# A hybrid mLSTM block on eight cores: weight casts in quarter pieces, branch weights by row blocks, q, k and v weights loaded apart, head 0 on two PSUM banks

## The reference, cut to what matters

```python
D_MODEL, BATCH, SEQ = 1024, 8, 4096          # 4 mLSTM heads of 256; SGU 8 groups x 128; FF 4096
def hybrid_layer(x, mod, ...):
    sh1, sc1, g1, sh2, sc2, g2 = split(mod, 6)           # mod = silu(c) @ w_ada + b_ada
    z = modulate(rmsnorm(x, norm1_g), sh1, sc1) @ w_in   # (S, 8208)
    qk, v_a, o_a, u_b, v_b, mg_pre, if_pre = split(z)    # 2048, 1024, 1024, 1024, 1024, 2048, 16
    qk = silu(centred_conv(qk, conv_w, conv_b))          # 3 taps over the sequence
    hA = mlstm_bidirectional(q, k, v, gates)             # forward scan + backward scan, per head
    y_a = rms_per_head(hA) * mh_g * sigmoid(o_a)
    y_b = spatial_gating(gelu(u_b), gelu(v_b), ln_v_g, ln_v_b, w_s, b_s)   # LayerNorm of v, 128 x 128 mixing
    mix = sigmoid(gate_a) * y_a + sigmoid(gate_b) * y_b
    x = x + g1 * (mix @ w_out)
    h2 = modulate(rmsnorm(x, norm2_g), sh2, sc2)
    return x + g2 * (square(relu(h2 @ w1)) @ w2)
out = rmsnorm(hybrid_layer(x, ...), normf_g)
```

## Time and profile before

| | |
|---|---|
| three runs | 2501.6, 2508.23 and 2832.83 us, median 2508.23 us |
| profiled execution | 2501.95 us; span of the slowest core (core 2) 2500.4 us |
| spans of the cores | 2469.1 to 2500.4 us |
| busy share of the span | PE 89%, DVE 56%, ACT 45%, POOL 36% |
| instructions | 49035, of them 15024 matmuls |
| DMA | 221.77 MB, mean 89 GB/s; casts on POOL's queue 29.66 MB |

### The profile page before, as it was taken

One profiled execution on the slowest core, in us unless ns is written; L12 is line 12 of the kernel. 1 busy time (PEld: TensorE's weight loads), 2 busy tenths in 40 slices (PEclk: granted clock), 3 DMA queues, 4 the chain that ended last, 5 costly groups with the idle time before them and its releaser, 6 DMA issues.

```text
span 2500.4 us, 49035 instructions; the slowest of 8 cores (2469.1 to 2500.4 us)
## 1 busy us (share of the span) xinstructions
PE 2237.1 (89%) x15024; PEld 1339.4 (54%) x15024; DVE 1410.4 (56%) x3059; ACT 1126.3 (45%) x2268; POOL 902.1 (36%) x1081
## 2 busy tenths in 40 slices
PE   3589949987848999999997899999999999999997
PEld 0245424444434655555553456666666666666664
DVE  1368738775546887887886863333333333333332
ACT  1355524445535766676664543333333333333332
POOL 2155625510112665665666651221222222222211
PEclk9899979998978999999998999999999999999998
DMA  7643463203685555455515552111111111111110
GB/s 220 187 156 124 101 89 104 100 30 31 77 99 72 110 108 123 102 104 132 113 55 173 187 184 69 51 52 51 52 52 51 51 45 44 41 43 44 51 35 34
DMA packets 145370, 221.77 MB, mean 89 GB/s; under 512 B 14996, under 2 KB 95444, under 8 KB 141144
## 3 DMA queue, kind: packets, MB, share of 16 engines
q1 hardware_dynamic: 108504, 188.98, 23.9%
q0 software_dynamic: 36608, 29.66, 11.3%
HBM read 197.90 MB, written 79.71 MB: 111 GB/s over the span
## 4 chain that ended last, share of the span: by engine, by line
PE 67%; DVE 9%; DMA 8%; issue 7%; SPq 4%; ACT 2%; POOL 2%; DVEq 0%; ACTq 0%; POOLq 0%
PE ps L355 66%; DVE arena L395 6%; SPq L348 4%; DMA mix_d<-arena 2%; ACT arena L375 2%; DMA hf_d<-arena 2%; PE ps L367 2%; POOL arena L390 2%; DMA arena<-w_in 1%; DMA wg_d<-w_in 1%; DVE arena L390 1%; DMA arena<-wg_d 1%; POOL arena L387 0%; DMA arena<-wq_d 0%; DVEq L1216 0%
## 5 line engine op out<-in xcount | busy, mean ns | idle before, releaser
L355 PE MATMUL ps<-arena 128*128 128x256 bf16 (+6 forms) x14000 | 2191.1, 323 | 227.6 <-ACT arena L375 79.1
L355 PEld LDWEIGHTS ps<-arena 128*128 128x128 bf16 (+1 forms) x14000 | 1278.0, 98 | 1102.2 <-issue 350.6
L390 POOL TENSOR_TENSOR arena<-arena 128x1 f32<-128x1 f32 (+3 forms) x654 | 707.3, 1089 | 1165.3 <-ACT arena L375 361.8
L395 DVE SCALAR_TENSOR_TENSOR arena<-ps,arena 128x256 bf16<-128x256 f32 (+6 forms) x1474 | 607.1, 414 | 668.0 <-ACT arena L375 509.5
L375 ACT ACTIVATE arena<-ps 128x256 f32<-128x256 f32 (+2 forms) x966 | 491.9, 523 | 862.8 <-PE ps L355 694.6
L375 ACT ACTIVATE arena<-arena 128x514 bf16<-128x514 f32 (+5 forms) x558 | 403.6, 733 | 336.7 <-DVE arena L395 92.7
L395 DVE SCALAR_TENSOR_TENSOR arena<-arena 128x256 bf16<-128x256 f32 (+2 forms) x257 | 284.2, 1107 | 80.9 <-DMA mix_d<-arena 43.8
L375 ACT ACTIVATE arena<-ps,arena 128x256 f32<-128x256 f32 (+3 forms) x512 | 255.4, 519 | 154.3 <-DMA hf_d<-arena 52.7
L390 DVE TENSOR_TENSOR arena<-ps,arena 128x512 bf16<-128x512 f32 (+4 forms) x294 | 169.9, 583 | 139.5 <-PE ps L355 136.5
L387 POOL TENSOR_SCALAR arena<-arena 128x1 f32<-128x1 f32 (+2 forms) x317 | 150.6, 477 | 192.5 <-ACT arena L375 140.4
L395 DVE SCALAR_TENSOR_TENSOR arena<-arena,ps 128x514 f32<-128x514 f32 x240 | 178.6, 744 | 35.6 <-PE ps L355 32.6
(11 more groups left out here) (16 smaller groups left out, 63.1 us busy)
## 6 DMA issues: line engine op xcount, KB each, us to landing
arena<-x SPq DMA_DIRECT2D x64, 512.0 KB, 4.6
arena<-w_ada SPq DMA_DIRECT2D x8, 2048.0 KB, 9.9
hf_d<-arena SPq DMA_DIRECT2D x128, 128.0 KB, 3.6
arena<-hf_d SPq DMA_DIRECT2D x128, 128.0 KB, 2.9
w_d<-w POOLq DMA_DIRECT2D x16, 1024.0 KB, 9.5
out<-arena SPq DMA_DIRECT2D x32, 512.0 KB, 3.5
arena<-w_d SPq DMA_DIRECT2D x13, 1024.0 KB, 5.6
arena<-w_in SPq DMA_DIRECT2D x6, 2048.0 KB, 33.1
```

The source lines that it names most:

```text
L355: ins = e.matmul(o_, l_, r_, start=st, stop=sp)
L390: return E(eng, lambda e, o_=o_, a_=a_, b_=b_, op=op: e.tensor_tensor(o_, a_, b_, op), reads, writes, 0.6 if op == ALU.pow else vcost(eng, ...
L395: e.scalar_tensor_tensor(o_, a_, sc, b_, op0, op1), reads, writes, vcost("dve", o_))
```

## The change

- The head casts are cut into four pieces each, by rows: `cast_next(after)` pops one of 80 quarters (256 rows x 256 columns). The mix stage calls it once per tile while `i + 3 < NT` (29 times), in order q, k, v of head 0, gates of head 0, q, k, v of head 1 and so on; the mLSTM stage calls it once per chunk pair (51 times), where it waits for the reciprocal of that pair (`pace=`, an ordering that marks no read). The quarters of one piece share a semaphore.
- When they are used up, the casts of w_out, w1 and w2 follow in 36 halves, one at every second pair.
- `wq_d` becomes three separate blocks of 128 x 8 x 256, `wqkv` three tiles, each with a load of its own; `halo_part` is done for q and for k apart, and `prep_part` takes the two q tiles first.
- In the lead-in the u and v weights are loaded by row blocks: eight loads of 128 rows x 2048 columns into the `wad` tiles, each as soon as its `w_ada` slice is used. The merge gate weights follow as four loads of 256 rows x 1024 columns. `cast_uv` and `cast_m` cast them; tile 0's projections run by row block over four banks. The small constants are loaded later, and the load of the LN gains (`lngb`) waits for row block 3, whose tile the last gate weight load reuses.
- In head 0 and block 0 of head 1, `next_bv` alternates `prep_v`, `prep_s` and `halo_part` between banks 2 and 3.

```diff
-            DMA("pool", dst, w_in[:, c0:c0 + 256].rearrange("(kc p) n -> p kc n", p=128), after, [rr], None)
+        for kind, h in (("q", 0), ("g", 0), ("q", 1), ("q", 2), ("g", 1), ("q", 3), ("g", 2), ("g", 3)):
+            for j in range(3 if kind == "q" else 2):
+                gs_ = new_dsem()
+                for m in range(4):
+                    head_casts.append((kind, h, j, m, gs_))
+            DMA("pool", dst, w_in[m * 256:(m + 1) * 256, c0:c0 + 256].rearrange("(kc p) n -> p kc n", p=128), [], [rr], gs_, pace=after)
...
-                if 20 <= i < 23:
-                    cast_piece("q", 0, i - 20, [R("ss", i)])
+                cast_next([R("ss", i + 3)])
...
+                    pace = [R("sml", (pctr[0] - 1) % NSM)]
+                    if not cast_next(pace) and pctr[0] % 2 and casts:
+                        dst, src, rr = casts.pop(0)
+                        DMA("pool", dst, src, [], [rr], None, pace=pace)
-                pace = [R("P", "F", (nxt % 8) % 2)]
-                for kind, h_, j_ in pieces[2 * nxt - 2:2 * nxt]:
-                    cast_piece(kind, h_, j_, pace)
...
-            DMA("sp", wqkv, wq_d[h], [R("wq_d", h, j) for j in range(3)], [R("wqkv")], wqkv_sem)
+            for p_ in range(3):
+                DMA("sp", wqkv[p_], wq_d[h][p_], [R("wq_d", h, p_, m) for m in range(4)], [R("wqkv", p_)], wqkv_sem[p_])
...
+        for kc in range(8):
+            DMA("sp", wad[kc], w_in[kc * 128:(kc + 1) * 128, 4096:6144], [], [R("wad", kc)], wasem[kc])
...
+        def load_m(n):
+            DMA("sp", wad[n].rearrange("p (k n) -> p k n", k=2), w_in[n * 256:(n + 1) * 256, 7168:8192].rearrange("(kc p) n -> p kc n", p=128),
+                [], [R("wad", n)], wasem[n])
...
-        DMA("sp", lgs, lngb, [R("B1b"), R("A1b")], [R("lgs")], new_dsem())
+        DMA("sp", lgs, lngb, [R("B1b"), R("A1b"), R("wad", 3)], [R("lgs")], new_dsem())
...
+        def next_bv(h, b):
+            vctr[0] += 1
+            return BV if h > 1 or (h == 1 and b > 0) or vctr[0] % 2 else BOG
```

More of the change, by code:

```diff
@@ L103, in op @@
                 add(rr)
+        for r in pace:
+            add(r.lw)
         o._excl = excl
@@ L277, in build_program @@
     hf_d = [nc.dram_tensor(f"hf{j}_d", [S, 256], F32, kind=sk).ap() for j in range(2)]
-    wq_d = [nc.dram_tensor(f"wq{j}_d", [128, 8, 768], BF16, kind=sk).ap() for j in range(4)]
+    wq_d = [nc.dram_tensor(f"wq{j}_d", [3, 128, 8, 256], BF16, kind=sk).ap() for j in range(4)]
     wg_d = [nc.dram_tensor(f"wg{j}_d", [128, 8, 512], BF16, kind=sk).ap() for j in range(4)]
@@ L714, in build_program @@
         ptr[0] = base_persist
-        wqkv_sem = new_dsem()
+        wqkv_sem = [new_dsem() for _ in range(3)]
         Chat, Cbf = {}, {}
```

189 lines of the change are left out of this document (104 added, 85 removed).

## The result

The changed kernel takes 2390.8 us in the median (2390.0 to 2395.1, 4 runs). Its ratio to the kernel before is 0.9548 (95% interval 0.9519 to 0.9577).

A forecast was written before the change was run, and what follows sets the result against it. Stores stuck behind whole casts were taken as the bound. On core 1, 2496.5 - 74.5 = 2422.0, + 3 (mix quarters) - 2 (weights) - 2 (bank) - 2 (lead-in) = 2419, forecast as 2420 us; range 2390 to 2462.

The forecast's parts named there:

- What bounds the kernel: Mix stage and head 0: stores landing with a cast stall the kernel, 41 and 58 us lost on core 2.
- B: Mix stage and head 0: quarters still stall, landing in over 6 us; 2470 us, no change; chance 0.13.
- F: Stalls come from bytes moved, not the burst; only small parts gain, 2490 us, no change; chance 0.08.
- Quarter casts, mix stage: Quarters land in 4.9 us; core 1 gets back its 31.2 us loss less 3 us of remaining DVE idle.
- Quarter casts, head 0: Stores fit the 8 us of two hfo buffers, so the whole loss returns: 43.3 us on core 1.
- The second bank: Head 0: a second PSUM bank cuts PE's idle time; 2 us gained (0 to 17).
- rival C: Head 0 bound by DVE or ACT once stores are gone: 19 us more, 2439; chance 0.70 with A and D.
- The loads apart: Heads: separate q, k, v weight loads can start earlier; 2 us gained (0 to 8) over three changes of head.
- Lead-in: Before the first tile's store: new load order puts the last m load at 133, 2 us back (-12 to +15).
- rival D: Lead-in: w_in's 8 KB rows run at the w_ada rate or better, ending 15 us earlier: 2405; 0.70 with A, C.
- The core that ends last: Core 1 sets the time: 2422.0 us after its 74.5 us of losses return, against 2401 for core 2.
- rival E: Heads 1 to 3: POOL blocked by casts; 0.9 us per pair eats the 88 us gain, 1.4 gives 2554; chance 0.05.

The follow-up runs named there:

- run with whole casts: Changed kernel with four quarters merged into one DMA of 1024 rows, every fourth tile or chunk pair: 2500 us, ratio to before 0.9943.
- run with doubles: Changed kernel, but from head 0 on two whole casts (1024 rows each) back to back every 8 chunk pairs: 2469.3 us, ratio to before 0.9796.
- casts alone: Kernel before with only the quarter casts; its whole w_out, w1 and w2 casts begin at block 13: 2429.4 us, ratio to before 0.9686.
- late start alone: Changed kernel with the first quarter issued at tile 4 instead of tile 0: 2411.6 to 2422.5 us; again on another chip, 2389.7 to 2395.7.

## Why the prediction was right in kind and 29 us too slow

**What bounds the kernel: right.** The stalls were stores that land with a cast. The run with whole casts brings back the mix stage's, the run with doubles a part of head 0's. Rivals B and F are out by the quarters' landing time and by the run with whole casts.

**Quarter casts, mix stage: right.** 31.2 less 3 us were forecast to come back on core 1. With the casts alone its mix stage fell from 403.7 to 380.6, 23 us (27 in the mean of the cores); with the whole change to 369.2, so that some 10 us of the 34 are not the casts'. The quarter's landing time of 4.9 us was met.

**Quarter casts, head 0: right in size, wrong in one part of the mechanism.** 43.3 us were forecast to come back on core 1; the casts alone bring 40 there and 41 in the mean. But the text had whole casts as such for the cause. It was their pairing: one alone costs 0.4 us there. Nor does every double stall: on core 2 of before the two casts issued at 656.55 and 657.36 landed within the clean second piece of the earlier trace rows, which the text itself calls a piece with three casts.

**The second bank: the step that failed.** "PE is idle 2.1 of 16 us in the clean piece, 17 us over 32 pairs for all causes; I take 2 (0 to 17)." It is worth 16 (12 to 14 counted from the run with the casts alone). The bound held, the choice inside it rested on no row: it called 2.1 of 16 us little, which is the very idle time that a second bank can take away (with one bank 22 us of head 0, with two 8), and left out what the clock gains with it. The clean pieces of the earlier trace rows ran with one bank, so their 4 us a pair was the pace of the bank: the runs with one bank have 4.3 and 4.1 over the 24 pairs, the changed kernel 3.75. That is below the pace at which rival C had DVE or ACT as the next bound, so C is out. Of the 29 us that the forecast was too slow, this term is 14.

**The loads apart: too small.** 2 us (0 to 8) were taken over three changes; the first alone has 5 to 9, of which 4 show in the medians. The 30 us of idle PE that bounded it were those of heads 1 to 3, and the first load stands at the end of head 0.

**Lead-in: about right by two errors.** 2 us were forecast, and the first store came 2 us earlier on core 1, 5.7 in the mean. The w_in rows did move faster, as rival D has it (271 GB/s in the stretch below, on core 2, where the earlier trace rows has 159; but core 2 was the slowest of before, whose cores had 159 to 209 there, and those of the changed kernel have 269 to 286):

```profile
51.00:91.00 40.00, 20.05 (x64) 6.72 (x66) 11.87 (x18) 18.89 (x22) 13.07 (x7) 0.76 0.80 271
```

But the quarters of tiles 0 to 3, and the gains that came late beside them, took that back: the late start alone has the first store 10 us earlier, at 128.5, which is the 15 us and more under before (144.8) that D had. That the 2 us came out is luck. What could have been read ahead: the order puts those quarters beside loads that the whole start waits for.

**The core that ends last: half right.** Core 1 was taken to set the time. In the profiled execution core 4 did, and in the other three cores 1, 3 and 2; the profiled cores end within 13 us instead of 31. In heads 1 to 3 core 1 took 584.1 us before and 575.1 after; a lag seen in one profiled execution was taken for the core's own. Together, on core 1 against the forecast: 18 us more in head 0 (63.3 returned instead of 45.3 with the bank), 7 in heads 1 to 3 (9.0 instead of 2), 6 in the mix stage, and 6 in the gap behind it and the end of the heads make 37; core 4 ends 8 us later than core 1, which leaves 29.

**Hidden costs: rival E is out, the rest is open.** POOL's stretch of heads 1 to 3 rose from 354 to 387 us busy on core 2, and PE waited 6.9 us for POOL there, far from the 88 that E needs. That the half casts of w_out, w1 and w2 cost nothing is not shown: heads 1 to 3 took 573 us before, 576 after, and 567 with the casts alone.

The Trainium skill (DMA: Bandwidth & Descriptors, Rules for kernel authors) asks for DMAs of 1 MiB and over where bandwidth is the goal. Here 80 DMAs of 128 KB beat 20 of 512 KB, since what counts is the longest burst ahead of a small store. The Trainium skill (DMA: Bandwidth & Descriptors, Queues, rings and completion order) lets a DMA engine finish a whole packet of one queue before it turns to another. That stores wait longer behind wholes than behind halves agrees with it in direction; no run here looked at single packets.

## What to carry to other kernels

When a bulk DMA on one queue and small stores on another share the engines, compare the bulk DMA's landing time with the time until each store's buffer is wanted again, place by place: here the size cost next to nothing under it, above it stalls began and grew, and two in a row counted as one long one. A clean piece of the kernel before shows the pace of its own buffers too, so its idle time, and what the clock loses by it, is what a second buffer can bring, and must be priced and not waved off. When a background transfer is moved, look where the last of its train ends up: four quarters taken out of the lead-in came back as 10 us at the end of head 3.

## What the runs showed of the hardware

- A whole cast (1024 rows) landed in 14 to 20 us in the mix stage and in 10 to 12 in head 0, a quarter in 5 (the medians of the cores); of two whole ones back to back in head 0 the first in 14, the second in 20 and up to 27.
- Four casts of 128 KB beside loads on the other queue took these from 12.7 to 19.8 us (`w_in`, 1 MB) and from 15.7 to 27.3 (`lngb`).
- Dies and chips differ in what they grant a busy TensorE: 0.93 and 0.99 in the same stretch of the same kernel on two dies of one chip. The changed kernel took 2391, 2399 and 2421 us (medians) on three occasions.
